# Block kernel with experts: order of the last blocks, reads of the y rows, and whole weight loads

## The chip, the core and the metric

The kernel runs on one core of a Trainium2 chip. The metric is the time of one execution on the device in microseconds (us), the median of three runs. A profiled execution is taken by itself; its instructions are placed in microseconds from the start of its span.

## What is computed

One layer of a hybrid block on x of 512 tokens x 1024: a mixing half (a spatial gate beside stick-breaking attention), then a mixture of experts. All of what is changed lies in the second half:

```python
gates = route(h, w_router, router_bias)          # 64 experts, 8 of them per token, others 0
g = jnp.einsum('sd,edf->sef', hs, w_gate)        # 1024 -> 256 per expert
u = jnp.einsum('sd,edf->sef', hs, w_up)
act = jax.nn.silu(g) * u * gs[:, :, None]
routed = jnp.einsum('sef,efd->sd', act, w_down)  # 256 -> 1024
y = routed + (jax.nn.silu(h @ ws_gate) * (h @ ws_up)) @ ws_down
x = x + ga2 * rmsnorm(y, g_post_ffn)
```

All inputs are float32. The kernel splits an operand into a rounded high part and the rest ("low") and multiplies high x high, high x low and low x high.

## The kernel before, in words

**Blocks.** The experts are done sparsely. A block is one expert with up to 128 of its tokens. Blocks 0 to 63 are the experts in order. Where an expert has more than 128 tokens, further blocks follow at the end; `nover` of them were counted on the chip, and `npair` = m pairs are run. Here m = 2, 68 blocks. Blocks alternate between two sets of tiles (slots s = 0, 1).

**Tables.** `posb` and `vtab` hold a column per block: each token's place in the block and the values that give its row and gate. A fill loop on GpSimd (`fill_step`, L657 and L660) copies the columns of an over-full expert for its further blocks. `eid` names the expert of a block behind the 64th.

**One block.** SyncE loads gate and up weights (1 MB each) into `raw`, in two halves of the inner range: half 0 of gate and up, then half 1 (`load_half`, L472; 4 KB per partition and piece). `refill` issues a half when VectorE has subtracted the same half of the block two before. ScalarE rounds a half to `whi` (`high`, L858), VectorE computes `wlo` = raw - whi (`low`, L1791, semaphore `lo_dve`, two counts per block). GpSimd gathers the token rows (L622); TensorE transposes them (L1001), computes the place tables (L1297) and multiplies gate and up over k = 0 to 7 (`gate_up`, L1317 to L1319), waiting for `lo_dve` before k = 0 and again before k = 4. VectorE forms silu(g) x u x gate (L1798), TensorE transposes it (L1001) and multiplies with the down weights (`down`, L1335 and L1341); these are loaded by ScalarE's queue (L905) and split at L910 and L1815. ScalarE takes the result out (`ysb`, L901) and GpSimd scatters its rows (L630).

**The y rows.** `y_rows` in DRAM has 4096 rows of 1024: row 8 x token + rank, where the rank counts the token's selected experts in the order of their numbers. After the last block SyncE waits for all scatters and reads everything back into `yall` (16 MB, laid over the tiles of the blocks), in 8 transfers: for each row group t of 128 tokens ranks 0 to 3, then ranks 4 to 7 (L526). Then per row group: TensorE sums the shared expert's rows `ysh` and ranks 0, 1, 2, 4 with an identity matrix (`part_sum`, L1421); VectorE adds ranks 5, 6, 7 to rank 3 (L1887), then TensorE's sum (L1889); ScalarE squares the result (L992); VectorE multiplies it by ga2 (L1891), works out the norm's factor (`factor`, L1448 to L1456, with ScalarE's root, L708) and adds to x (L1898). SyncE writes the output (L531).

**Order.** Each engine's order is written out by hand: `step_dve`, `step_act`, `step_pool` and `block_pe` do a part of several neighbouring blocks each. `step_dve` of block b: row table of b-3, place table of b+2, low part of b's token rows, of the down weights of b-2, one-hot of b+3, the low part of the activations of b-2, `low` of b, and `times_up` of b-1. `block_pe` of b: transposes of b+1, tables of b+3, gate/up products of b, down products of b-1. SyncE's queue holds the refills, and after the last one the reads of y.

Of the kernel before, what the change touches and what calls it, by code (L numbers as in the profile page):

```python
# [24 lines left out]
I32 = mybir.dt.int32  # L25
# [29 lines left out]
COLS = E + OVER + 6  # L55
# [3 lines left out]
HC = 1024  # L59
# [3 lines left out]
def block_kernel(nc, x, c, w_ada, b_ada, g_pre_mix, w_in, ln_sgu_g, ln_sgu_b, w_spatial, b_spatial,  # L63
                 g_branch, w_out, g_post_mix, g_pre_ffn, w_router, router_bias, w_gate, w_up,
                 w_down, ws_gate, ws_up, ws_down, g_post_ffn, out):
    with ExitStack() as ctx:
# [19 lines left out]
        yall = at("yall", [P, TT, TOPK, D], F32, 0)  # L86
# [123 lines left out]
        eid = small("eid", [1, E + OVER], I32)  # L210
        offs = small("offs", [P, OVER], F32)
# [114 lines left out]
        scatter_go = sem("scatter_go")  # L326
        gathered = [sem(f"gathered{s}") for s in range(SLOTS)]
# [18 lines left out]
        y_in = [sem(f"y_in{t}_{g}") for t in range(TT) for g in range(2)]  # L346
        ypart_mm = sem("ypart_mm")
        root_set = sem("root_set")
        ysum_ok = sem("ysum_ok")
# [10 lines left out]
        y_v = y_rows.rearrange("(t p r) n -> t p r n", r=TOPK, p=P)  # L360
# [31 lines left out]
        Y_BANK = [0, 2, 6, 0]  # L392
        Y_PE, Y_DVE = (0, 1, 2, 4), (5, 6, 7)
# [38 lines left out]
        def _(sp):  # L432
# [36 lines left out]
            def load_half(e, s, half):  # L469
                cols = slice(half * HC, (half + 1) * HC)  # L470
                for m_, w in enumerate((wg_v, wu_v)):
                    sp.dma_start(raw[:, s, m_, cols], w[bass.ds(e, 1)].rearrange("e p f -> p (e f)")[:, cols])\  # L472
                      .then_inc(gu_in[s][half], 16)

            def load_gate_up(e, s):
                for half in range(2):
                    load_half(e, s, half)
# [26 lines left out]
            def refill(i, s, e):  # L504

                b = num(*after(i, s, -2))
                for half in range(2):
                    sp.wait_ge(lo_dve, b * 2 + (1 + half))
                    load_half(e, s, half)

            with sp.Fori(2, E // 2) as i:
                for s in range(SLOTS):
                    refill(i, s, num(i, s))
            sp.wait_ge(over_ok, 1)
            m = sp.value_load(npair[0:1, 0:1], min_val=0, max_val=OVER // 2)
            with sp.If(m > 0):
                with sp.Fori(E // 2, m + E // 2) as i:
                    for s in range(SLOTS):
                        e = sp.value_load(eid[0:1, bass.ds(num(i, s), 1)], min_val=0, max_val=E - 1)
                        refill(i, s, e)  # L520

            for s in range(SLOTS):
                sp.wait_ge(scattered[s], m * 16 + 16 * (E // 2))
            for t in range(TT):
                for g in range(2):
                    sp.dma_start(yall[:, t, 4 * g:4 * g + 4], y_v[t][:, 4 * g:4 * g + 4]).then_inc(y_in[2 * t + g], 16)  # L526
# [9 lines left out]
        def _(gp):  # L536
# [21 lines left out]
            gp.iota(eid[:, 0:E], [[1, E]], base=0, channel_multiplier=0)  # L558
            then(gp.iota(iote[:, :], [[0, 1]], base=0, channel_multiplier=1, allow_small_or_imprecise_dtypes=True))
# [94 lines left out]
            with gp.If(n > 0):  # L654
                with gp.Fori(0, n) as j:
                    e = gp.value_load(eid[0:1, bass.ds(j + E, 1)], min_val=0, max_val=E - 1)
# [5 lines left out]
            gp.sem_inc(fill_step, 1)  # L662
            gp.wait_ge(fill_step, n * 2 + 1)
            gp.sem_inc(fill_ok, 1)
            step_pool(1, 1)
            m = gp.value_load(npair[0:1, 0:1], min_val=0, max_val=OVER // 2)
# [13 lines left out]
        def _(ac):  # L680
# [171 lines left out]
            def high(i, s, half):  # L852
                ac.wait_ge(gu_in[s][half], i * 32 + 32)
                if half == 0:
                    if not (isinstance(i, int) and i == 0):
                        ac.wait_ge(gu_mm, num(i, s) - 1)
                cols = slice(half * HC, (half + 1) * HC)
                A(whi[:, s, :, cols], raw[:, s, :, cols], ACT.Copy).then_inc(hi_ok, 1)  # L858
# [107 lines left out]
            with ac.Fori(3, E // 2) as i:  # L966
                for s in range(SLOTS):
                    step_act(i, s, 3)
            ac.wait_ge(over_ok, 1)
            m = ac.value_load(npair[0:1, 0:1], min_val=0, max_val=OVER // 2)  # L970
            with ac.If(m > 0):
# [958 lines left out]
```

## Time and profile before

| | us |
|---|---|
| median of 3 runs | 1081.46 (1081.21 to 1082.55) |
| profiled execution, its own time | 1087.6 |
| its span | 1085.9 |
| TensorE busy | 1027.3 |
| VectorE busy | 858.2 |
| ScalarE busy | 648.0 |
| GpSimd busy | 287.3 |

In the profile PE is TensorE's products, PEld its weight loads, DVE VectorE, ACT ScalarE, POOL GpSimd, SP SyncE; L12 is line 12 of the kernel. A float32 product of 128x512 stands as two passes (records). The share of busy time is an average over stages: the mixing half and the routing take the first 350 us, the blocks run to about 1028 us, the sum of the y rows is the rest. PEclk is the clock granted to TensorE as a share of 2.4 GHz. "Idle before" is how long the engine idled before an instruction, and what ended that.

### The profile page before, as it was taken

The page shows a single profiled execution, that of the slowest core. Times are in us where ns is not written, and L with a number is a line of the kernel's source. Part 1 is how long each engine was busy: PE and PEld are TensorE (multiplying, and loading weights), DVE is VectorE, ACT ScalarE, POOL GpSimd, SP SyncE. Part 2 cuts the span into 40 slices and gives each one's busy share as a digit, 9 for nine tenths or more (in the row PEclk, how much of TensorE's full clock was granted, in tenths as well). Part 3 has the DMA queues.
Part 4 walks back from the last instruction along what each step waited for, and adds up shares of the span by engine and source line. Part 5 has one row for each costly group of instructions (what it writes and reads, how often), then busy time and mean ns, then how long its engine had stood idle before and what let it go on. Part 6 is the DMA issues. An engine that isn't in the chain of part 4 may idle for free.

```text
span 1085.9 us, 15632 instructions
## 1 busy us (share of the span) xinstructions
PE 1027.3 (95%) x4668; PEld 744.5 (69%) x4668; DVE 858.2 (79%) x1412; ACT 648.0 (60%) x743; POOL 287.3 (26%) x220
## 2 busy tenths in 40 slices
PE   4998999899998999999999999999999999999866
PEld 0786776568755777777777777777777777777632
DVE  1669766644778898888898899989899999999447
ACT  5334135742443777677677677777677777777501
POOL 1232221540303432222221232233123223322200
PEclk9899998999999999999999999999999999999989
DMA  9666752112344899999999999999999999999297
GB/s 338 253 244 260 262 169 93 61 37 107 103 189 163 311 374 370 364 365 367 384 364 384 356 366 364 380 371 368 365 363 352 350 357 357 354 360 334 84 394 301
DMA packets 87495, 318.67 MB, mean 293 GB/s; under 512 B 19312, under 2 KB 19824, under 8 KB 77360
## 3 DMA queue, kind: packets, MB, share of 16 engines
q1 hardware_dynamic: 53232, 200.30, 50.6%
q10 hardware_dynamic: 11616, 72.66, 17.4%
q0 software_dynamic: 22624, 45.40, 11.3%
q8 instruction: 13, 0.21, 0.1%
q14 instruction: 10, 0.08, 0.0%
HBM read 317.25 MB, written 39.85 MB: 329 GB/s over the span
## 4 chain that ended last, share of the span: by engine, by line
PE 56%; DMA 24%; DVE 11%; ACT 4%; issue 3%; SPq 1%; ACTq 1%; DVEq 0%; POOL 0%; POOLq 0%
DMA raw<-in_w_up_dram 18%; PE ps L1317 7%; PE ps L1319 7%; PE ps L1318 7%; PE ps L1335 6%; PE ps L1091 6%; PE ps L1341 5%; PE ps L1001 5%; DMA yall<-y_rows 4%; DVE wlo L1791 3%; PE ps L1193 2%; ACT whi L858 2%; PE ps L1175 2%; PE ps L1017 2%; PE ps L1142 1%
## 5 line engine op out<-in xcount | busy, mean ns | idle before, releaser
L1791 DVE TENSOR_TENSOR wlo<-raw,whi 128x2048 fp32r<-128x2048 f32 x136 | 307.8, 2287 | 34.0 <-ACT whi L858 34.0
L858 ACT ACTIVATE whi<-raw 128x2048 fp32r<-128x2048 f32 x136 | 261.0, 1920 | 73.2 <-DMA raw<-in_w_up_dram 72.8
L1317 PE MATMUL ps<-whi,hthi 128*128 128x512 f32 x544 | 224.6, 413 | 0.0
L1319 PE MATMUL ps<-whi,htlo 128*128 128x512 f32 x544 | 212.8, 391 | 0.0
L1318 PE MATMUL ps<-wlo,hthi 128*128 128x512 f32 x544 | 212.6, 391 | 0.0
L630 POOL DMA_INDIRECT y_rows<-ysb,idxs x68 | 69.1, 1016 | 461.1 <-DVE idxg L1785 432.4
L622 POOL DMA_INDIRECT hg<-h_rows,idxg x70 | 129.5, 1850 | 70.4 <-DVE idxg L1785 50.2
L901 ACT ACTIVATE ysb<-ps 128x1024 f32<-128x1024 f32 x68 | 69.7, 1025 | 107.2 <-PE ps L1341 107.1
L1335 PE MATMUL ps<-rawd,actt 128*128 128x512 f32 x272 | 127.7, 592 | 1.5 <-ACT actt L894 1.5
L1319 PEld LDWEIGHTS ps<-whi,htlo 128*128 128x128 f32 x544 | 102.1, 188 | 22.8
L1318 PEld LDWEIGHTS ps<-wlo,hthi 128*128 128x128 f32 x544 | 102.6, 189 | 17.0
L1317 PEld LDWEIGHTS ps<-whi,hthi 128*128 128x128 f32 x544 | 102.2, 188 | 17.1
L1805 DVE TENSOR_TENSOR htlo<-ps,hthi 128x1024 fp32r<-128x1024 f32 x68 | 83.3, 1225 | 10.7 <-ACT hthi L890 10.7
L1815 DVE TENSOR_TENSOR wdlo<-rawd,wdhi 128x1024 fp32r<-128x1024 f32 x68 | 82.7, 1216 | 1.5 <-ACT wdhi L910 1.5
L1341 PE MATMUL ps<-wdhi,acth 128*128 128x512 f32 x136 | 80.9, 595 | 0.0
L1335 PEld LDWEIGHTS ps<-rawd,actt 128*128 128x128 f32 x272 | 51.1, 188 | 39.7 <-issue 32.7
L1001 PE MATMUL ps<-ident,hg 128*128 128x128 f32 x552 | 71.7, 273 | 0.5 <-DVE eid L1754 0.4
L910 ACT ACTIVATE wdhi<-rawd 128x1024 fp32r<-128x1024 f32 x68 | 72.1, 1061 | 0.0
L890 ACT ACTIVATE hthi<-ps 128x1024 fp32r<-128x1024 f32 x68 | 69.4, 1021 | 2.8 <-PE ps L1001 2.8
L1001 PEld LDWEIGHTS ps<-ident,hg 128*128 128x128 f32 x552 | 64.3, 140 | 9.4 <-DVE eid L1754 0.5
L1770 DVE TENSOR_SCALAR s_onehot<-iotab,posb 128x128 bf16<-128x128 bf16 x284 | 62.1, 284 | 0.0
L1473 DVE SCALAR_TENSOR_TENSOR acc<-ada,sc_col,acc 128x1024 f32<-128x1024 f32 x35 | 53.0, 1515 | 3.8 <-DMA ada<-in_w_ada_dram 2.7
(270 smaller groups left out, 1614.7 us busy)
## 6 DMA issues: line engine op xcount, KB each, us to landing
raw<-in_w_gate_dram SPq DMA_DIRECT2D x136, 512.0 KB
raw<-in_w_up_dram SPq DMA_DIRECT2D x136, 512.0 KB
rawd<-in_w_down_dram ACTq DMA_DIRECT2D x66, 1024.0 KB
ada<-in_w_ada_dram SPq DMA_DIRECT2D x24, 1024.0 KB, 8.6
yall<-y_rows SPq DMA_DIRECT2D x8, 2048.0 KB, 22.9
wraw<-in_w_in_dram POOLq DMA_DIRECT2D x8, 1024.0 KB, 5.7
woraw<-in_w_out_dram SPq DMA_DIRECT2D x16, 256.0 KB, 2.8
xs<-in_x_dram SPq DMA_DIRECT2D x4, 512.0 KB, 6.0
```

Of the source, the lines that this page charges most:

```text
L622: gp.indirect_dma_start(out=hg[s][:, :, :].rearrange("p k q -> p (k q)"), out_offset=None, in_=h_rows, in_offset=bass.IndirectOffsetOnAxis ...
L858: A(whi[:, s, :, cols], raw[:, s, :, cols], ACT.Copy).then_inc(hi_ok, 1)
L910: A(wdhi[s][:, :, :], rawd[:, s, :, 0:DC], ACT.Copy).then_inc(wdhi_ok, 1)
L1001: return pe.transpose(o, i, ident[:, :])
L1317: mm(out_, hthi[s][:, k, :], hi, start=(k == 0), stop=False)
L1318: mm(out_, hthi[s][:, k, :], lo, start=False, stop=False)
L1319: ins = mm(out_, htlo[s][:, k, :], hi, start=False, stop=(k == KD - 1))
L1335: mm(bank(5), actt[:, k, :], rawd[:, s, k, DC:D], start=(k == 0), stop=(k == KF - 1))
L1341: ins = mm(bank(4), a_[:, k, :], w, start=(k == 0 and j == 0), stop=(k == KF - 1 and j == 2))
L1791: V.tensor_tensor(wlo[s][:, :, c0:c1], raw[:, s, :, c0:c1], whi[:, s, :, c0:c1].bitcast(F32), ALU.subtract).then_inc(lo_dve, 1)
L1805: V.tensor_tensor(htlo[s][:, :, :], bank(0, 2).rearrange("p (k q) -> p k q", k=KD), hthi[s][:, :, :].bitcast(F32), ALU.subtract).then_inc( ...
L1815: V.tensor_tensor(wdlo[:, s, :, 0:DC], rawd[:, s, :, 0:DC], wdhi[s][:, :, :].bitcast(F32), ALU.subtract)\
```

## The change

- The further blocks of over-full experts come after block 55, before the last eight experts (`MID` = 56, `LASTE` = 8). To this end GpSimd copies the table columns of experts 56 to 63 behind those of the further blocks, and their numbers into `eid`; from block 56 on SyncE and ScalarE read the expert from `eid`, and VectorE's `onehot` takes columns shifted by 8.
- Gate and up are loaded, rounded and subtracted whole, one after the other, instead of in two halves of both. TensorE waits for both subtractions before k = 0.
- The y rows are read rank by rank into tiles `yr0` to `yr7` that lie over tiles of the last blocks: rank 0 after block 66's subtractions (numbers as with 68 blocks), ranks 1 and 2 after its gate/up products, rank 3 after block 67's subtractions, ranks 4 and 5 after its gate/up products, ranks 6 and 7 after the last down products, by row group. Before the read of rank r SyncE also waits until the block of expert 56 + r is scattered.
- VectorE adds the shared rows to rank 0, then ranks 1, 2, 3, 5. TensorE sums rank 4, VectorE's sum, ranks 6 and 7. ScalarE squares TensorE's sum out of PSUM. The product with ga2 reads PSUM too and stands behind the variance.

```diff
@@ names and tiles
+LASTE = 8
+MID = E - LASTE
+COLS = E + OVER + LASTE + 6
-        yall = at("yall", [P, TT, TOPK, D], F32, 0)
+        yr = [at(f"yr{r}", [P, TT, D], F32, (0, 48, 96, 16, 64, 80, 32, 112)[r] * KB) for r in range(TOPK)]
-        y_v = y_rows.rearrange("(t p r) n -> t p r n", r=TOPK, p=P)
+        y_v = y_rows.rearrange("(t p r) n -> p t r n", r=TOPK, p=P)
-        Y_BANK = [0, 2, 6, 0]
-        Y_PE, Y_DVE = (0, 1, 2, 4), (5, 6, 7)
+        Y_BANK = [0, 2, 4, 6]
+        Y_DVE = (1, 2, 3, 5)
@@ SyncE
+            def load_one(e, s, m_):
+                sp.dma_start(raw[:, s, m_, :], (wg_v, wu_v)[m_][bass.ds(e, 1)].rearrange("e p f -> p (e f)"))\
+                  .then_inc(gu_in[s][m_], 16)
...
+            def rank_done(r):
+
+                pairs = (MID + r) // 2
+                sp.wait_ge(scattered[r % 2], m * 16 + 16 * (pairs + 1))
+                sp.sem_inc(read_go, 1)
+
+            def read_rank(r):
+                sp.dma_start(yr[r][:, :, :], y_v[:, :, r]).then_inc(y_in[r], 16)
+
+            for r in range(4):
+                rank_done(r)
+            sp.wait_ge(lo_dve, m * 4 + 2 * (E - 2) + 2)
+            sp.sem_inc(read_go, 1)
+            read_rank(0)
+            sp.wait_ge(gu_mm, m * 2 + (E - 1))
+            sp.sem_inc(read_go, 1)
+            read_rank(1)
+            read_rank(2)
+            sp.wait_ge(lo_dve, m * 4 + 2 * (E - 1) + 2)
+            sp.sem_inc(read_go, 1)
+            read_rank(3)
+            sp.wait_ge(gu_mm, m * 2 + E)
+            sp.sem_inc(read_go, 1)
+            rank_done(4)
+            read_rank(4)
+            rank_done(5)
+            read_rank(5)
+            sp.wait_ge(dn_mm, m * 2 + E)
+            sp.sem_inc(read_go, 1)
+            rank_done(6)
+            rank_done(7)
+            for t in range(TT):
+                for r in (6, 7):
+                    sp.dma_start(yr[r][:, t, :], y_v[:, t, r]).then_inc(y_last[t], 16)
@@ GpSimd, behind the fill loop
+            gp.tensor_copy(posb[:, :, bass.ds(m * 2 + E, LASTE)], posb[:, :, MID:E]).then_inc(fill_step, 1)
+            gp.tensor_copy(vtab[:, :, bass.ds(m * 2 + E, LASTE), :].rearrange("p t b v -> p t (b v)"),
+                           vtab[:, :, MID:E, :].rearrange("p t b v -> p t (b v)")).then_inc(fill_step, 1)
+            gp.tensor_copy(eid[:, bass.ds(m * 2 + MID, LASTE)], elast[:, :]).then_inc(fill_step, 1)
@@ ScalarE
+                A(whi[:, s, m_, :], raw[:, s, m_, :], ACT.Copy).then_inc(hi_ok, 1)
...
-                ac.wait_ge(ysum_ok, t + 1)
-                A(junk[:, :], yall[:, t, 3, :], ACT.Square, accum_out=stat[:, ST_S, t:t + 1]).then_inc(sumsq, 1)
+                ac.wait_ge(ypart_mm, t + 1)
+                A(junk[:, :], bank(Y_BANK[t], 2), ACT.Square, accum_out=stat[:, ST_S, t:t + 1]).then_inc(sumsq, 1)
@@ TensorE
                 if k0 == 0:
                     pe.wait_ge(htlo_ok, num(i, s) + 1)
+                    pe.wait_ge(lo_dve, num(i, s) * 2 + 2)
                 for k in range(k0, k1):
-                    if k == 0 or k == KH:
-                        pe.wait_ge(lo_dve, num(i, s) * 2 + 1 + k // KH)
...
+            def add_rows(t, rows, first=False, last=False):
+                for hf in range(2):
+                    ins = mm(bank(Y_BANK[t] + hf), ident[:, :], rows[:, hf * 512:(hf + 1) * 512], start=first, stop=last)
+                return ins
+
+            pe.wait_ge(y_in[4], 16)
+            for t in (0, 1, 3, 2):
+                if t == 2:
+                    pe.wait_ge(y_ok, m * 2 + E)
+                add_rows(t, yr[4][:, t, :], first=True)
+            for t in range(TT):
+                pe.wait_ge(dsum_ok, t + 1)
+                add_rows(t, yr[0][:, t, :])
+                pe.wait_ge(y_last[t], 32)
+                add_rows(t, yr[6][:, t, :])
+                add_rows(t, yr[7][:, t, :], last=True).then_inc(ypart_mm, 1)
@@ VectorE
+            def shared_rank0(t):
+                y = yr[0][:, t, :]
+                then(V.tensor_tensor(y, y, ysh[t][:, :], ALU.add))
+
+            v.wait_ge(y_in[0], 16)
+            shared_rank0(0)
+            shared_rank0(1)
             times_up(last, 1)
             down_low(last, 1)
             rows_of(last, 0)
+            shared_rank0(2)
             act_low(last, 1)
             rows_of(last, 1)
+            shared_rank0(3)
+            for r in Y_DVE:
+                v.wait_ge(y_in[r], 16)
+                for t in range(TT):
+                    y = yr[0][:, t, :]
+                    ins = V.tensor_tensor(y, y, yr[r][:, t, :], ALU.add)
+                    if r == Y_DVE[-1]:
+                        ins.then_inc(dsum_ok, 1)
+                    else:
+                        then(ins)
+            def weighted(t):
+
+                v.wait_ge(ypart_mm, t + 1)
+                return V.tensor_tensor(yr[0][:, t, :], bank(Y_BANK[t], 2), ga2[:, :], ALU.mult)
```

## Rows read from the trace of the kernel before

**Rows 1.** Chain that ended last, from 900 us on: start us, us, what.
```profile
1030.29 2.06 DMA y_rows<-ysb,idxs
...
1035.76 38.50 DMA yall<-y_rows
```

**Rows 2.** Busy us of each engine by stretch, then PEclk, DMA share, GB/s.
```profile
403.00:626.00 223.00, 218.79 (x1060) 165.63 (x1058) 193.62 (x330) 162.37 (x177) 58.18 (x44) 1.00 0.98 368
...
715.00:796.00 81.00, 79.58 (x387) 60.46 (x386) 70.37 (x121) 59.48 (x65) 21.07 (x16) 1.00 0.98 367
...
796.00:1014.00 218.00, 218.00 (x1058) 166.28 (x1057) 202.01 (x332) 161.03 (x177) 66.16 (x44) 1.00 0.94 343
```

**Rows 3.** Timeline of PE and DVE: start us, us, engine line op, idle before.
```profile
614.51 0.48 PE L1317 MATMUL ps<-whi,hthi 128*128 128x512 f32 x1
...
615.31 2.29 DVE L1791 TENSOR_TENSOR wlo<-raw,whi 128x2048 fp32r<-128x2048 f32 x1 [3.50 <-ACT whi L858]
...
626.02 0.48 PE L1317 MATMUL ps<-whi,hthi 128*128 128x512 f32 x1
...
989.30 4.49 DVE L1791 TENSOR_TENSOR wlo<-raw,whi 128x2048 fp32r<-128x2048 f32 x2
...
994.38 0.48 PE L1317 MATMUL ps<-whi,hthi 128*128 128x512 f32 x1
```

**Rows 4.** Waits of the whole run: us in total, times, longest us.
```profile
DVE wlo L1791 <- ACT whi L858: 34.0, 27, 3.5
```

**Rows 5.** DMA by queue, 403 to 615 us: packets, MB, share.
```profile
q1 hardware_dynamic: 12079, 43.99, 56.7%
...
q10 hardware_dynamic: 3024, 22.02, 26.8%
```

**Rows 6.** DMA by queue, 1034 to 1074 us.
```profile
q1 hardware_dynamic: 1224, 16.71, 98.9%
```

**Rows 7.** Timeline of the last blocks, POOL, DVE, PE and ACT.
```profile
995.56 1.02 POOL L630 DMA_INDIRECT y_rows<-ysb,idxs  x1 [6.65 <-DVE idxg L1785]
...
1001.50 2.28 DVE L1791 TENSOR_TENSOR wlo<-raw,whi 128x2048 fp32r<-128x2048 f32 x1
...
1020.03 1.88 PE L1335 MATMUL ps<-rawd,actt 128*128 128x512 f32 x4
...
1020.51 1.05 ACT L910 ACTIVATE wdhi<-rawd 128x1024 fp32r<-128x1024 f32 x1
...
1030.29 0.96 POOL L630 DMA_INDIRECT y_rows<-ysb,idxs  x1 [4.07 <-ACT ysb L901]
```

**Rows 8.** DMA issues of the whole run: KB each, us to landing.
```profile
rawd<-in_w_down_dram ACTq DMA_DIRECT2D x66, 1024.0 KB
...
y_rows<-ysb,idxs POOLq DMA_INDIRECT x68, 8.1
```

**Rows 9.** Timeline of DVE after the last block.
```profile
1024.94 0.43 DVE L1820 TENSOR_TENSOR actl<-actt,acth 128x256 fp32r<-128x256 f32 x1 [2.06 <-ACT acth L895]
...
1044.71 3.74 DVE L1887 TENSOR_TENSOR yall<-yall 128x1024 f32<-128x1024 f32 x3 [19.28 <-DMA yall<-y_rows]
```

**Rows 10.** Timeline of PE after the last block.
```profile
1039.78 9.26 PE L1421 MATMUL ps<-yall,ident 128*128 128x512 f32 x16 [9.65 <-DMA yall<-y_rows]
...
1050.59 7.03 PE L1421 MATMUL ps<-yall,ident 128*128 128x512 f32 x16
```

**Rows 11.** Busy us by stretch after the last block; the clock as PEclk.
```profile
1036.00:1040.00 4.00, 0.22 (x1) 0.23 (x2) 0.00 (x0) 0.00 (x0) 0.00 (x0) 0.50 1.05 446
```

**Rows 12.** Timeline of the last row group's end, ACT and DVE.
```profile
1079.38 1.06 ACT L992 ACTIVATE junk<-yall 128x1024 f32<-128x1024 f32 x1 [8.40 <-DVE yall L1889]
...
1082.04 1.41 DVE L1898 SCALAR_TENSOR_TENSOR xs<-yall,rs,xs 128x512 f32<-128x512 f32 x2
```

**Rows 13.** Timeline of POOL around the fill of the over-full blocks.
```profile
360.73 2.27 POOL L660 COPY vtab<-vtab  x1
...
374.50 1.02 POOL L630 DMA_INDIRECT y_rows<-ysb,idxs  x1 [6.49 <-DVE idxg L1785]
```

## What is predicted

> **What bounds the kernel now.** I read the chain that ended last first, then the busy time by stretch, then the timelines of the last blocks. The chain's end [rows 1] shows a tail that starts when the last block's scatter is done: 1030.29 + 2.06 = 1032.35 us. Only then does SyncE read the 16.8 MB of y rows back, 38.50 us of pure transfer in the chain, and the span ends 53.5 us after the scatter landed. In that time TensorE and VectorE mostly wait or add rows. Before it, over 68 blocks, TensorE is full: from 796 to 1014 us it is busy for 218.00 of 218.00 us at a period of 9.91 us, while from 403 to 626 and from 715 to 796 us it loses 4.2 and 1.4 us with the DMA engines at 0.98 [rows 2]. So in the middle TensorE bounds and the weight loads come close to it; there is at most 5.6 us to win there. What the tail holds is much more.
>
> **Tail, part by part.** The change reads rank r of all 512 tokens (2.10 MB) as soon as the tile under it is used up. That is allowed since rank r of a token can't lie in a later expert than 56 + r, and the last eight blocks are now experts 56 to 63.
>
> 1. First issue. Rank 0 waits for block 66's second weight subtraction, which ends at 1001.50 + 2.28 = 1003.8 us [rows 7]; the scatter of block 63, the last of the four that SyncE waits for, is issued at 995.56 [rows 7] and lands some 8.1 us later [rows 8], at the same time. SyncE's refills are all issued 10 us before, so nothing of them stands behind the new waits. So 28.5 us of the 53.5 us head start are won in principle.
>
> 2. What has to flow before rank 4 is in. TensorE begins with rank 4, and SyncE's queue runs in order, so ranks 0 to 4 come first: 5 x 2.10 = 10.5 MB. Beside them go two down loads of 1.05 MB [rows 8] and three scatters of blocks 64 to 66, 64 rows x 4 KB = 0.26 MB each: 13.4 MB in all. The latency from issue to use: the first VectorE add began at 1044.71 [rows 9], 12.4 us after 1032.35, for 4.19 MB, which at the rate of [rows 6] are 9.9 us; 2.4 us remain.
>
> 3. The rate. Reads of y rows before had runs of 16 KB and made 16.71 MB / (0.989 x 40 us) = 422 GB/s [rows 6]. The new ones have runs of 4 KB, as the halves of the gate and up loads do: 43.99 / (0.567 x 212) = 366 GB/s while they mix with scatters and gathers [rows 5]. These two are the bounds. I take 395, the middle: 4 KB runs, but little beside them. Rank 4 is in at 1003.8 + 2.4 + 33.9 = 1040.1 us (1037.9 by the fast bound, 1042.8 by the slow one). The Trainium skill (DMA: Bandwidth & Descriptors, Specifications) gives about 358 GB/s as the HBM limit of a core; by it rank 4 would be in at 1043.6 us and the end 3.5 us later than in my sum. Behind that rule: the trace does not agree, the tail's row shows 422 GB/s.
>
> 4. TensorE then adds rank 4 for four row groups, 16 passes. It will have idled some 11 us after the last down product. Before, after a similar wait the granted clock was 0.50, the 1.2 GHz level, when the adds began [rows 11], and the first 16 passes took 9.26 us where a later 16 took 7.03 us [rows 10]. So rank 4 ends at 1049.3 us.
>
> 5. Next, per row group: VectorE's sum, rank 6, rank 7, 12 passes, 48 in all: 3 x 7.03 = 21.1 us, to 1070.5 us. Are their inputs there? VectorE adds the shared rows in the gaps of the last block, then 16 adds (ranks 1, 2, 3, 5) of 3.74 / 3 = 1.25 us [rows 9] from about 1026.6 us, after the last act_low and one more shared add. The adds of ranks 1 to 3 run to 1041.6 us. Rank 5 lands at 1003.8 + 2.4 + 15.7 MB / 0.395 = 1046.0 us and the first sum is ready at 1047.3, 2 us before TensorE asks. Ranks 6 and 7 of group 0 land near 1049 us, of group 3 near 1057 us, where TensorE asks at 1067. The last scatter is issued at 1030.29 [rows 7]; amid the reads it may land several us later than before, but SyncE's own queue is full until 1046. So **TensorE is late next**: its adds come one behind the other from 1040 us.
>
> 6. After TensorE: before, from the start of the last Square (1079.38) to the span's end took 6.5 us [rows 12]. Square now reads PSUM instead of the sum. VectorE's add from PSUM (1.2 us) goes away. The product with ga2, which ran beside Square, now comes after it, inside the wait for the root: +1.0 us. So 7.5 us: the end is 1070.5 + 7.5 = 1078.0 us against 1085.9: **7.9 us less** (bounds of the rate: 10.0 and 5.2; a clock that stays up adds 2.2).
>
> The down load of block 67, issued after the down products of block 65, now shares the engines with ranks 1 to 3. Its first use was at 1020.51 us [rows 7]. If it is 5 us late, the last down product moves from 1028 to 1033, and TensorE waits for rank 4 until 1040 anyway: nothing.
>
> **Middle.** (a) Gate and up are loaded whole, 8 KB runs instead of 4 KB. The down loads have had 8 KB runs all along: 22.02 / (0.268 x 212) = 388 GB/s against 366 for the gate and up halves in the same stretch [rows 5]. That is 5.4 us instead of 5.7 us of DMA time per block, 0.3 of about 10. In the two late stretches blocks take 10.1 us instead of 9.87, so this gain alone is about what is lacking; bounds zero and the full 5.6 us. (b) TensorE now waits for both subtractions before its first gate/up product. In an undisturbed block the second ends at 989.30 + 4.49 = 993.79, 0.6 us before the products start at 994.38 [rows 3]: hidden, and this slack is all the cover there is. In a late block it isn't: at 615.31 + 2.29 = 617.6 the second one ends 3.1 us after the start at 614.51 [rows 3]. Before, only the products from k = 4 waited (the next block's began 11.5 us on, at 626.02, 1.6 us late); now all of the 3.1 us stand. All waits of this kind sum to 34.0 us in 27 places [rows 4]. I don't expect this sum: while the loads set the pace, the blocks' ends are given by the DMA rate, and starting later costs the lost cover (2.5 to 3 us) once per stretch, two stretches, 5 us. With (a) taking most of the lateness away, I put (a) and (b) together at **3 us less**, between 5.6 less and 5 more.
>
> **Costs at nothing.** Over-full blocks ahead of the last eight: the same 68 blocks, the same loads. The experts read from a table in 12 blocks instead of 4: SyncE and ScalarE did it in the four last ones before, in the stretch without a stall [rows 2]. Three more copies and an iota on GpSimd: the copies there took up to 2.27 us [rows 13], it idles 6.5 us before its scatter one block on, and the gather behind them is needed a block later still.
>
> **Sum.** 7.9 + 3 = 10.9 us. The profiled execution has 1087.6 us around a span of 1085.9; the median of the runs is 1081.46, 6 us less. The tail's part should carry over; of the stalls in the middle fewer may exist there, which I leave within the range. 1081.46 - 10.9 = **1070.6 us**.
>
> **Rivals.**
> - R1, the lost cover outweighs the wide loads: middle 2 to 5 us more, tail as above: 1075.5 to 1079. For it: the slack of 0.6 us [rows 3]. Against: the 388 against 366 GB/s. Chance 0.14.
> - R2, TensorE pays every late subtraction, since its delay moves the next block's subtractions and loads too: 34.0 us less the 5.6 already lost, +28: about 1102. It decides once the middle loses over 8 us. Against: the last third has no late block. Chance 0.05.
> - R3, the strided rank reads are slow, **ending slower than before**: rows of 4 KB at 32 KB from token to token and 4 MB from row group to row group. At half my rate (0.198 MB/us) the 16.8 MB take 85 us, with 8 us for the rest; ranks 6 and 7 would land at 1099, and 3.5 + 7.5 us of adds and end give 1110 in the span: about 1106. It decides below 277 GB/s. Against: the before reads step by 32 KB between tokens too. The Trainium skill (DMA: Bandwidth & Descriptors, Latency and other measured facts) reports copies falling to about half at a row pitch of 4 MiB per partition; no run here shows that, and the 4 MB step here lies between row groups of one partition. Chance 0.05.
> - R4, better than the sum: fast bound of the rate, clock kept up, stalls all gone and a little more: 18 to 22 us less, 1060 to 1063.5. Chance 0.07.
> - R5, the early reads don't start early, since a scatter's landing holds SyncE behind the whole chain of waits: each wait is in order, so one late scatter delays all ranks behind it. 5 to 8 us of the tail's gain lost: 1076 to 1080. Chance 0.04.
> - Forecast: tail 5 to 12 less, middle 0 to 5.6 less. Chance 0.65.
>
> About 0.2% (2.2 us) is what a measurement of this kernel can tell from no change. Faster: 0.65 + 0.07 + most of R1 and R5 = 0.86; same 0.04; slower 0.10. The range, 1063 to 1078, holds the forecast and most of R1, and leaves out R2, R3, nearly all of R4.
>
> **What would show it.** Step 1: first y read issued near 1004 us, before the last block's products. Steps 2 and 3: y reads landing in order at 395 GB/s. Step 4: TensorE's rank 4 adds begin near 1040 us at a low clock. Step 5: from 1049 us TensorE without a gap for 21 us, VectorE's waits for DMA before it. Middle: second weight subtractions ending before the products in most blocks, TensorE idle under 3 us between 403 and 1014. I am wrong if TensorE waits for VectorE or the DMA after 1050 us, or if its idle time in the middle grows.

## The result, and the profile after

| | before | after |
|---|---|---|
| median, runs on the same chip | 1082.01 (1081.21 to 1083.09, 4 runs) | 1071.05 (1069.88 to 1075.07, 4 runs) |
| ratio | | 0.9905, 95% interval 0.9877 to 0.9932 |
| profiled execution, its own time | 1087.6 | 1075.07 |
| its span | 1085.9 | 1073.0 |

The kernel is faster by 11.0 us at the medians; forecast were 10.9 us and 1070.6. To see where they came from I cut each span at two marks that every kernel here has: the start of the gate/up products of block 2 and of the last block. What lies between them, 66 blocks, I call the middle, what follows the tail.

Timeline of TensorE after, the two marks and the adds of the y rows (start us, us, engine line operation, idle before):

```profile
363.59 0.47 PE L1348 MATMUL ps<-whi,hthi 128*128 128x512 f32 x1
...
1009.30 0.47 PE L1348 MATMUL ps<-whi,hthi 128*128 128x512 f32 x1
...
1035.94 29.68 PE L1442 MATMUL ps<-yr,ident 128*128 128x512 f32 x64 [11.80 <-DMA yr<-y_rows]
```

Before, the same marks stand at 363.54 and 1014.21 us, with the span's end at 1085.9. So the middle went from 650.7 to 645.7 us, **5.0 less**, and the tail from 71.7 to 63.7 us, **8.0 less**. The forecast was 3 and 7.9. Together that is 13.0 us in one pair of profiles (the spans differ by 12.9); the medians show 11.0, with an interval of 7 to 13.

One profile is one execution. In the six kernels that are the same up to the last block (this one and e5 to e9 below) the middle took 642.9 to 645.8 us. With e1 that makes seven kernels with whole loads, at 642.9 to 647.1; the two with the loads and waits of before took 650.7 and 651.2 (e4). So a gain in the middle is clear, its size only to some 2 us. The tail repeats better: 71.3 to 71.7 us in the four kernels that have the tail of before, 63.1 (e6) and 64.2 (e8) in two that have the changed one but for one detail.

**The middle after.** Busy us by stretch (PE, PEld, DVE, ACT, POOL, each with its instructions, then PEclk, DMA share, GB/s), to be laid beside [rows 2]:

```profile
403.00:626.00 223.00, 221.99 (x1079) 169.35 (x1078) 203.96 (x339) 164.75 (x180) 67.89 (x46) 1.00 0.97 376
...
715.00:796.00 81.00, 80.89 (x392) 61.58 (x391) 74.34 (x128) 60.06 (x68) 24.39 (x17) 1.00 0.98 377
796.00:1014.00 218.00, 218.00 (x1058) 166.47 (x1057) 199.39 (x323) 157.72 (x174) 65.43 (x43) 1.00 0.93 349
```

TensorE's idle time in the two late stretches fell from 4.2 to 1.0 and from 1.4 to 0.1 us. The costliest groups of instructions on the page (busy us, mean ns of one, idle before) no longer show a wait at the subtractions, where [rows 4] had 34.0 us, nor at the roundings:

```profile
L1821 DVE TENSOR_TENSOR wlo<-raw,whi 128x2048 fp32r<-128x2048 f32 x136 | 305.2, 2285 | 0.0
L891 ACT ACTIVATE whi<-raw 128x2048 fp32r<-128x2048 f32 x136 | 261.4, 1923 | 0.0
```

DMA by queue, 403 to 615 us (packets, MB, share of 16 engines), beside [rows 5]: gate and up on q1 now move at 45.07 / (0.547 x 212) = 389 GB/s, where the 4 KB halves made 366, and close to the 388 of the down loads on q10 before.

```profile
q1 hardware_dynamic: 6189, 45.07, 54.7%
```

**The tail after.** Chain that ended last, from 1000 us on (start us, us, what), beside [rows 1]. Where 38.50 us of transfer stood in front of everything, 20.38 us stand now, and then TensorE works:

```profile
1015.52 20.38 DMA yr<-y_rows
1035.94 29.70 PE ps L1442 x64
1065.67 1.12 ACT junk L1024 x2
...
1066.97 1.14 DVE yr L1935
...
1069.10 0.75 DVE xs L1942
```

SyncE, its waits from 988 to 1001.2 us (us in total, times, longest), then its timeline:

```profile
SPq L527 <- DMA y_rows<-ysb,idxs: 10.5, 2, 9.6
```

```profile
1000.60 0.38 SPq L530 DMA_DIRECT2D yr<-y_rows  x1
...
1005.47 3.69 SPq L530 DMA_DIRECT2D yr<-y_rows  x3
```

The first read is issued at 1000.60 us, the next three from 1005.47 on. VectorE's timeline shows what the first one waited for besides the scatters, and the adds that follow:

```profile
994.38 4.49 DVE L1821 TENSOR_TENSOR wlo<-raw,whi 128x2048 fp32r<-128x2048 f32 x2
...
1023.50 15.12 DVE L1926 TENSOR_TENSOR yr<-yr,yr 128x1024 f32<-128x1024 f32 x12
1041.80 4.63 DVE L1926 TENSOR_TENSOR yr<-yr,yr 128x1024 f32<-128x1024 f32 x4 [3.18 <-DMA yr<-y_rows]
```

Block 66's second subtraction ends at 994.38 + 4.49 = 998.87 us, 1.7 us before the read is issued: in between, SyncE was still held by the scatter of block 63.

DMA by queue, 1004 to 1040 us: the reads on q1 made 12.76 / (0.888 x 36) = 399 GB/s.

```profile
q1 hardware_dynamic: 3218, 12.76, 88.8%
q10 hardware_dynamic: 144, 1.05, 7.5%
```

Stretches around the start of TensorE's adds; the third figure from the right is the granted clock:

```profile
1030.00:1035.00 5.00, 0.00 (x0) 0.00 (x0) 4.86 (x5) 0.00 (x0) 0.00 (x0) 0.50 1.03 413
1035.00:1040.00 5.00, 4.06 (x5) 1.85 (x6) 3.55 (x3) 0.00 (x0) 0.00 (x0) 0.51 1.02 407
1040.00:1045.00 5.00, 5.00 (x13) 2.23 (x12) 3.20 (x3) 0.00 (x0) 0.00 (x0) 1.00 1.03 411
```

The clock is at 0.50, the 1.2 GHz level, after 11.80 us of idling and while the first adds run: 5 passes in 4.06 us. From 1040 us on it is at 2.4 GHz: 13 passes in 5 us.

### The profile page after: what moved, and what is told of

Read it like the earlier page. It is cut to its first block, busy times and chain, and to the rows that moved or that the text cites. A ratio compares the mean times of both kernels' runs of the same rounds, so it can differ in the third digit from the quotient of the medians.

```text
span 1073.0 us, 15239 instructions
## 1 busy us (share of the span) xinstructions
PE 1019.2 (95%) x4652; PEld 743.2 (69%) x4652; DVE 870.5 (81%) x1416; ACT 644.7 (60%) x743; POOL 299.5 (28%) x224
## 4 chain that ended last, share of the span: by engine, by line
PE 80%; DMA 9%; DVE 7%; ACT 2%; issue 1%; ACTq 0%; SPq 0%; POOL 0%; DVEq 0%; POOLq 0%
PE ps L1348 11%; PE ps L1350 11%; PE ps L1349 11%; PE ps L1366 10%; PE ps L1033 8%; PE ps L1372 8%; PE ps L1123 6%; DMA hg<-h_rows,idxg 6%; PE ps L1442 3%; PE ps L1225 2%; DMA yr<-y_rows 2%; PE ps L1207 2%; PE ps L1049 2%; PE ps L1174 1%; PE ps L1285 1%
## 5 line engine op out<-in xcount | busy, mean ns | idle before, releaser
L661 POOL DMA_INDIRECT y_rows<-ysb,idxs x68 | 69.0, 1015 | 444.9 <-DVE idxg L1816 389.6
L653 POOL DMA_INDIRECT hg<-h_rows,idxg x70 | 140.3, 2005 | 71.0 <-DVE idxg L1816 50.5
## 6 DMA issues: line engine op xcount, KB each, us to landing
raw<-in_w_gate_dram SPq DMA_DIRECT2D x68, 1024.0 KB, 10.9
raw<-in_w_up_dram SPq DMA_DIRECT2D x68, 1024.0 KB, 12.9
rawd<-in_w_down_dram ACTq DMA_DIRECT2D x66, 1024.0 KB, 10.1
```

Of the source, the lines that this page charges most:

```text
L653: gp.indirect_dma_start(out=hg[s][:, :, :].rearrange("p k q -> p (k q)"), out_offset=None, in_=h_rows, in_offset=bass.IndirectOffsetOnAxis ...
```

## Experiments

Two questions: do the middle and the tail gain what the spans say, each by its own part of the change, and which resource sets the tail? Nine kernels were run. All do the whole computation; e6 adds products that are not needed. The runs of before beside them had medians of 1082.19 us (e1 to e4), 1082.40 (e5 to e8) and 1082.75 (e9).

**e1, the wide loads alone.** The kernel before, with whole loads of gate, then up, their roundings and subtractions whole, and TensorE waiting for both subtractions.

```diff
-            def load_half(e, s, half):
-                cols = slice(half * HC, (half + 1) * HC)
-                for m_, w in enumerate((wg_v, wu_v)):
-                    sp.dma_start(raw[:, s, m_, cols], w[bass.ds(e, 1)].rearrange("e p f -> p (e f)")[:, cols])\
-                      .then_inc(gu_in[s][half], 16)
+            def load_half(e, s, m_):
+                sp.dma_start(raw[:, s, m_, :], (wg_v, wu_v)[m_][bass.ds(e, 1)].rearrange("e p f -> p (e f)"))\
+                  .then_inc(gu_in[s][m_], 16)
...
+                    pe.wait_ge(lo_dve, num(i, s) * 2 + 2)
                 for k in range(k0, k1):
-                    if k == 0 or k == KH:
-                        pe.wait_ge(lo_dve, num(i, s) * 2 + 1 + k // KH)
```

> The kernel before with the whole gate and up loads and the one wait for both subtractions; order of blocks, y reads and sums as before. Theory (8 KB runs make the loads fast enough, nothing is lost by the wait): VectorE never waits for a rounded half (0 instead of 34.0 us), TensorE idles under 2 us between 403 and 1014 us, span 1080 to 1082, 3 to 5 us less than before. Rival (the middle's gain in the changed kernel came from the new order of the blocks): waits of 30 us or more remain and the time is that of before or 2 to 5 us more.

Measured: 1078.17 us, ratio 0.9958 (0.9941 to 0.9975), 4.0 us less at the medians. The page's group of the subtractions, and the stretch 403 to 626 us:

```profile
L1786 DVE TENSOR_TENSOR wlo<-raw,whi 128x2048 fp32r<-128x2048 f32 x136 | 305.2, 2284 | 0.0
```

```profile
403.00:626.00 223.00, 221.57 (x1067) 167.44 (x1066) 202.56 (x333) 163.85 (x179) 59.95 (x45) 1.00 0.97 373
```

The waits are gone and TensorE idles 1.4 instead of 4.2 us. The middle took 647.1 us (before 650.7), the tail 71.4 (before 71.7). So this part by itself makes most of the middle's gain and next to nothing in the tail.

**e2, the lost cover alone.** The kernel before, halves as they were, only TensorE's wait changed:

```diff
+                    pe.wait_ge(lo_dve, num(i, s) * 2 + 2)
                 for k in range(k0, k1):
-                    if k == 0 or k == KH:
-                        pe.wait_ge(lo_dve, num(i, s) * 2 + 1 + k // KH)
```

> The kernel before, only that TensorE waits for both weight subtractions before its first gate/up product; loads in 4 KB halves as before. Theory (the DMA engines set the pace in the late stretches, the lost cover is paid once per stretch): 2 to 6 us more than before. Rival (R2 of the prediction: each late subtraction is paid for): 20 to 28 us more. Second rival (a late TensorE leaves the DMA engines time to catch up, nothing is paid): within 1 us of before.

Measured: 1089.07 us, ratio 1.0061 (1.0038 to 1.0084), 6.9 us more than the median of before; the middle grew by 4.3 us to 655.0. Waits of its whole run:

```profile
PE ps L1316 <- DVE wlo L1790: 10.0, 8, 1.9
...
DVE wlo L1790 <- ACT whi L858: 16.2, 10, 2.9
```

TensorE waits in 8 places, 10.0 us in total. The 34.0 us of late subtractions do not turn into 34 us of waits of TensorE, and VectorE's own are down to 10 places and 16.2 us. This refutes R2's price (28 us) and bears out that of step (b) of the middle, about 5 us.

**e3, the width of the runs.** As e1, but each matrix comes in two transfers with 4 KB per partition: gate, gate, up, up.

```diff
-                sp.dma_start(raw[:, s, m_, :], (wg_v, wu_v)[m_][bass.ds(e, 1)].rearrange("e p f -> p (e f)"))\
-                  .then_inc(gu_in[s][m_], 16)
+                for half in range(2):
+                    cols = slice(half * HC, (half + 1) * HC)
+                    sp.dma_start(raw[:, s, m_, cols],
+                                 (wg_v, wu_v)[m_][bass.ds(e, 1)].rearrange("e p f -> p (e f)")[:, cols])\
+                      .then_inc(gu_in[s][m_], 16)
```

> As the kernel with whole loads only, but each matrix in two transfers with runs of 4 KB: gate first, then up, one wait, narrow runs. If the width of the runs makes the gain: VectorE's waits for ScalarE come back (over 20 us) and the time is as with both waits alone. If it is that gate is loaded whole before up (or fewer waits at SyncE): 3 to 5 us less than before, as with the whole loads.

Measured: 1082.69 us, ratio 0.9997 (0.9979 to 1.0016), the same as before. Waits of its whole run:

```profile
DVE wlo L1789 <- ACT whi L858: 17.7, 15, 2.6
...
PE ps L1316 <- DVE wlo L1789: 8.6, 10, 1.9
```

Against e1 the pieces are half as wide, and there are four transfers of 512 KB per block instead of two of 1 MB: 1082.69 - 1078.17 = 4.5 us. So the wide loads pay; whether by their 8 KB runs or by their fewer and larger transfers no run here tells apart. Against e2 the width, the transfers and the wait for both subtractions are the same. Only the order differs (gate whole before up, and so too the roundings and subtractions), and e3 is 6.4 us faster by time (2.9 us in the middles, 652.1 and 655.0). So the order counts too: it takes back what the merged wait cost. How it does so stays open, since the waits of the two are nearly alike (17.7 and 16.2, 8.6 and 10.0 us). e1's 4.0 us are then the sum of three steps: + 6.9 for the merged wait (e2), - 6.4 for the order, - 4.5 for the wide loads.

**e4, the tail alone.** The changed kernel with halves, two roundings over both and the two waits of before.

```diff
-                sp.dma_start(raw[:, s, m_, :], (wg_v, wu_v)[m_][bass.ds(e, 1)].rearrange("e p f -> p (e f)"))\
-                  .then_inc(gu_in[s][m_], 16)
+                cols = slice(half * 1024, (half + 1) * 1024)
+                for m_, w in enumerate((wg_v, wu_v)):
+                    sp.dma_start(raw[:, s, m_, cols], w[bass.ds(e, 1)].rearrange("e p f -> p (e f)")[:, cols])\
+                      .then_inc(gu_in[s][half], 16)
...
-                    pe.wait_ge(lo_dve, num(i, s) * 2 + 2)
                 for k in range(k0, k1):
+                    if k == 0 or k == KH:
+                        pe.wait_ge(lo_dve, num(i, s) * 2 + 1 + k // KH)
```

> The changed kernel with the loads, the subtractions and TensorE's two waits in halves again, as before. Theory (tail and middle add up): 8 us less than before, about 1074, 3 us more than the changed kernel; the last gate/up product ends near 1020 us and from there to the end it takes 58 us. Rival (the new order of blocks alone changed the middle): within 1 us of the changed kernel.

Measured: 1076.06 us, ratio 0.9929 (0.9903 to 0.9955). The subtractions' group on its page has the waits of before again:

```profile
L1826 DVE TENSOR_TENSOR wlo<-raw,whi 128x2048 fp32r<-128x2048 f32 x136 | 307.9, 2286 | 37.6 <-ACT whi L894 37.6
```

The forecast was 8 us less than before. Its middle took 651.2 us, as before (650.7), its tail 65.8, 2.1 more than the changed kernel's. Most of that lies in the reads: the one of rank 0 took 11.9 us from issue to landing instead of 9.1, and rank 4's adds begin 28.4 us after the last block's products instead of 26.6. Why the reads are slower behind the halves wasn't tested. At the medians e4 saves 6.1 and e1 4.0 us, 10.1 together, by the ratios 7.7 and 4.5, 12.2 together; the whole change saves 11.0 by the one and 10.3 by the other. Within the intervals the two parts add up.

**e5, no early start.** The changed kernel, with all reads behind the last scatter; VectorE's adds of the shared rows go behind its work on the last block, as they would lock up otherwise.

```diff
             sp.sem_inc(read_go, 1)
-            read_rank(0)
...
             rank_done(6)
             rank_done(7)
+            read_rank(0)
+            read_rank(1)
+            read_rank(2)
+            read_rank(3)
+            read_rank(4)
+            read_rank(5)
```

> The changed kernel, but all reads of the y rows are issued after the last scatter; ranks, tiles, sums and loads as changed. Theory (the tail's gain is the early start, and TensorE's adds come one behind the other after rank 4): rank 4 is in at about 1057 us, then 9.3 + 21.1 + 7.5 us: a span of about 1095, 20 to 23 us more than the changed kernel and so about 9 more than before. Rival (the gain is the new sharing of the sums, the early start is hidden): within 5 us of the changed kernel.

Measured: 1090.74 us, ratio 1.0078 (1.0057 to 1.0098). TensorE's timeline, and DMA by queue from 1030 to 1050 us, where nothing but these reads runs:

```profile
1051.58 29.45 PE L1442 MATMUL ps<-yr,ident 128*128 128x512 f32 x64 [33.12 <-DMA yr<-y_rows]
```

```profile
q1 hardware_dynamic: 2051, 8.19, 102.4%
```

The early start is worth 1090.74 - 1071.05 = 19.7 us (18.7 by the ratios, as the two were not measured side by side), and the rest of the tail's change without it loses more than it brings: the kernel is slower than before although it keeps the wide loads. TensorE starts 47.1 us after the last block's products began, instead of 26.6. And the reads alone, 4 KB at a time with 32 KB from token to token and 4 MB from row group to row group, run at 8.19 / 20 = 409 GB/s. R3 is refuted: counted the same way, without the share, the 16 KB reads of [rows 6] made 16.71 / 40 = 418 GB/s.

**e6, the clock kept up.** The changed kernel, with 10 needless products (20 passes) between the last down product and the wait for rank 4; their result is overwritten.

```diff
+            for n in range(10):
+                mm(bank(0), ident[:, :], ga2[:, 0:512], start=True, stop=True)
             pe.wait_ge(y_in[4], 16)
```

> The changed kernel with ten needless products (20 passes) between the last down products and the wait for rank 4, into a bank that is overwritten. Theory (the clock's fall costs 2.2 us in the rank 4 adds, and the rest of the tail follows TensorE): 16 passes take 7.1 us instead of 9.2, the span is 2 us less. Rival (VectorE's sums or the last reads hold the start of the row groups): 0 to 0.5 us less, TensorE then waits for VectorE at 1043 us.

Measured: 1071.12 us, ratio 0.9892 (0.9871 to 0.9913), no gain over the changed kernel. TensorE's timeline, VectorE's, and the stretches around the start of the adds:

```profile
1021.03 8.74 PE L1446 MATMUL ps<-ga,ident 128*128 128x512 f32 x20
1032.34 29.43 PE L1442 MATMUL ps<-yr,ident 128*128 128x512 f32 x64 [2.56 <-DMA yr<-y_rows]
```

```profile
1038.45 4.63 DVE L1928 TENSOR_TENSOR yr<-yr,yr 128x1024 f32<-128x1024 f32 x4 [2.79 <-DMA yr<-y_rows]
```

```profile
1032.00:1034.00 2.00, 1.66 (x4) 0.95 (x5) 1.97 (x2) 0.00 (x0) 0.00 (x0) 0.93 1.02 406
1034.00:1036.00 2.00, 2.00 (x3) 0.73 (x3) 1.63 (x2) 0.00 (x0) 0.00 (x0) 0.50 1.02 408
1036.00:1038.00 2.00, 2.00 (x4) 0.73 (x3) 0.00 (x0) 0.00 (x0) 0.00 (x0) 0.71 1.03 412
```

The idle time before the adds fell from 11.80 to 2.56 us, but the clock was not kept up: it is at 2.4 GHz when the adds begin, falls to 1.2 GHz within 2 us although TensorE works, and is back between 1036 and 1038 us. So the 64 passes take 29.43 instead of 29.68 us, and the experiment does not do what it was made for. What a steady clock would give I can only work out: the 80 passes of e7 below take 34.49 us, 0.431 each, so 64 would take 27.6, 2.1 us less. VectorE's first sum would be in time for that: here it is ready at 1038.45 + 4.63 / 4 = 1039.6 us, 7.3 us after the adds began, as the first 16 passes would end (7.03 us in [rows 10]).

**e7, another sharing.** If TensorE's 64 passes behind rank 4 set the end, it should begin with rank 1, which lands earlier. TensorE adds ranks 1, 3, 4, then 7 and VectorE's sum (80 passes); VectorE adds ranks 2, 5, 6.

```diff
-        Y_DVE = (1, 2, 3, 5)
+        Y_DVE, Y_PE = (2,), (1, 3, 4)
...
-            pe.wait_ge(y_in[4], 16)
-            for t in (0, 1, 3, 2):
-                if t == 2:
-                    pe.wait_ge(y_ok, m * 2 + E)
-                add_rows(t, yr[4][:, t, :], first=True)
+            for r in Y_PE:
+                pe.wait_ge(y_in[r], 16)
+                for t in (0, 1, 3, 2):
+                    if r == Y_PE[0] and t == 2:
+                        pe.wait_ge(y_ok, m * 2 + E)
+                    add_rows(t, yr[r][:, t, :], first=(r == Y_PE[0]))
```

> The changed kernel with the adds shared differently: TensorE takes ranks 1, 3 and 4 as they come from 1024 us on, then only rank 7 and VectorE's sum per row group; VectorE takes ranks 2, 5 and 6. Theory (TensorE's 21 us of adds behind rank 4 set the end): rank 4 done at 1045 us, four groups of 3.5 us to 1059, end at 1067 us, 6 us less than the changed kernel. Rival (the DMA engines or VectorE set the end): 0 to 2 us less, TensorE waits for VectorE's sums after 1045 us.

Measured: 1066.72 us, ratio 0.9857 (0.9841 to 0.9874), 4.3 us below the changed kernel: it is faster than both kernels. The forecast was 6 us. TensorE's timeline, then VectorE's from its last add of rank 6 on:

```profile
1021.72 34.49 PE L1442 MATMUL ps<-yr,ident 128*128 128x512 f32 x80
```

```profile
1047.74 1.23 DVE L1932 TENSOR_TENSOR yr<-yr,yr 128x1024 f32<-128x1024 f32 x1 [0.94 <-DMA yr<-y_rows]
...
1048.95 1.21 DVE L1937 TENSOR_TENSOR yr<-ps,ga 128x1024 f32<-128x1024 f32 x1
...
1052.56 1.22 DVE L1937 TENSOR_TENSOR yr<-ps,ga 128x1024 f32<-128x1024 f32 x1
...
1056.17 1.22 DVE L1937 TENSOR_TENSOR yr<-ps,ga 128x1024 f32<-128x1024 f32 x1
...
1059.79 1.22 DVE L1937 TENSOR_TENSOR yr<-ps,ga 128x1024 f32<-128x1024 f32 x1
```

TensorE has 80 passes instead of 64 and is done at 1056.2 us, 51.1 us after the last block's products began, instead of 56.3. The bound is now VectorE: its last adds wait for the DMA and it then needs 3.6 us per row group, one behind the other. The tail took 60.8 us. Part of the gain may be the clock: TensorE's adds start at 2.4 GHz here, without a wait in front of them.

**e8, rank 0 earlier.** The changed kernel, where the read of rank 0 waits for the scatter of block 60 only (experts 56 to 59 are blocks 60 to 63).

```diff
-            for r in range(4):
-                rank_done(r)
+            rank_done(0)
...
             read_rank(0)
+            for r in range(1, 4):
+                rank_done(r)
```

> The changed kernel, but the read of rank 0 waits for the scatter of block 60 alone; the waits for blocks 61 to 63 stand behind it. Theory (the first read was held 1.6 us by the scatter of block 63, and all reads follow in order): the first read is issued at 999 us, rank 4 is in 1.6 us earlier, the span is 1 to 1.6 us less. Rival (ranks 1 to 5 are held by their own waits): rank 4 is in at the same time, no change.

Measured: 1069.98 us, ratio 0.9879 (0.9857 to 0.9902), the same as the changed kernel. SyncE's timeline and TensorE's:

```profile
993.73 10.16 SPq L530 DMA_DIRECT2D yr<-y_rows  x4
```

```profile
1004.00 0.47 PE L1349 MATMUL ps<-whi,hthi 128*128 128x512 f32 x1
...
1030.67 30.14 PE L1443 MATMUL ps<-yr,ident 128*128 128x512 f32 x64 [11.65 <-DMA yr<-y_rows]
```

The read starts 10.3 us before the last block's products instead of 8.7, as the forecast had it for the change. But the adds of rank 4 begin 26.7 us after them, as in the changed kernel (26.6). The earlier read moved hardly anything ahead. Counted from 12 us before the last block's products, all queues had moved 3.54 MB by 1 us before them (changed kernel: 3.47 MB), and 6.94 MB by 8 us after them (6.96 MB). Ranks 1 and 2 can't be issued before TensorE has left their tiles: rank 1 goes out 3.8 us before the last products in both kernels, and in the changed one the DMA share dips between that and the last products:

```profile
1008.30:1009.30 1.00, 1.00 (x13) 0.97 (x12) 0.99 (x3) 0.69 (x1) 0.00 (x0) 1.00 0.72 258
```

That the issue of rank 1 sets when rank 4 is in fits both kernels, but no run moved it by itself.

**e9, VectorE relieved.** As e7, with rank 3 back on VectorE and rank 6 of the last two row groups on TensorE. The edit is shown against the changed kernel.

```diff
-        Y_DVE, Y_PE = (2,), (1, 3, 4)
+        Y_DVE, Y_PE = (2, 3), (1, 4)
...
+                if t >= 2:
+                    add_rows(t, yr[6][:, t, :])
                 add_rows(t, yr[7][:, t, :])
```

> The kernel with the adds shared differently, one step further: VectorE, which idled 11.8 us before rank 5, also takes rank 3, and TensorE takes rank 6 of the last two row groups. Theory (in the first balance VectorE's chain of sums and norms, 3.6 us per row group behind 1049 us, set the end): 2 to 3 us less than the first balance, 1064 us, the end 7.5 us after TensorE's last pass. Rival (the work is balanced already, the last reads set the end): within 0.5 us of the first balance, 1066.7 us.

Measured: 1066.57 us (1063.36 to 1069.49), ratio 0.9858 (0.9834 to 0.9882). TensorE's timeline:

```profile
1019.22 7.03 PE L1442 MATMUL ps<-yr,ident 128*128 128x512 f32 x16
...
1029.03 7.13 PE L1442 MATMUL ps<-yr,ident 128*128 128x512 f32 x16 [2.77 <-DMA yr<-y_rows]
1036.49 17.48 PE L1442 MATMUL ps<-yr,ident 128*128 128x512 f32 x40 [0.33 <-DMA yr<-y_rows]
```

In its profile the tail is 58.5 us, 2.3 less than in e7. TensorE's last pass ends at 1053.97 us, 51.1 us after the last block's products began as in e7, but the span now ends 7.4 us behind it instead of 9.7: VectorE's chain of sums no longer sets the end. By time it is no faster than e7, in runs 6 us apart, and 1064 was forecast. Whether the 2.3 us are real is not decided.

## Why the prediction was right

The sum held: 10.9 us forecast, 11.0 measured, and both parts were found by themselves (e1 and e4). That it held to 0.1 us is luck: the interval is 7 to 13 us, the one pair of profiles shows 13.0, and in the middle the sum has no term for the order of the loads (6.4 us), which took back a cost of the merged wait that was larger than forecast. The mechanism of the tail, an early start of the reads and then TensorE's adds one behind the other, is shown by e5 and e7. Step by step:

- **Tail, step 1, first issue.** Forecast: at the subtractions of block 66, 10.4 us before the last block's products. Measured: 8.7 us before, held 1.7 us by the scatter of block 63. I had both ending at the same time; the scatter took longer to land. e8 takes 1.6 of the 1.7 us back and shows that they were worth nothing.
- **Steps 2 and 3, data and rate.** Forecast 395 GB/s with rank 4 in 25.9 us after the products' start (1040.1 - 1014.21). Measured 399 GB/s and 26.6 us. From the first issue to the adds of rank 4 I had 2.4 + 33.9 = 36.3 us, and it took 1035.94 - 1000.60 = 35.3. So a start 1.7 us late and a flow 1.0 us shorter leave 0.7 us; the rate makes 0.3 of that 1.0, the rest I can't assign. What the sum lacked is that the reads do not flow freely from rank 0 on, since ranks 1 and 2 wait for their tiles (e8). The Trainium skill (HBM Reference, Specifications (TRN2)) adds to the 358 GB/s that I weighed that a core which streams alone goes well above it; the 399 to 422 GB/s of this case's tails agree with that.
- **Step 4, rank 4 at a low clock.** Forecast a granted clock of 0.50 and 9.3 us for 16 passes. Measured 0.50 until 1040 us, and 9.1 us for them. That a clock kept up adds 2.2 us (R4) was not shown: e6 didn't keep it up. From e7's passes it would be 2.1.
- **Step 5, TensorE is late next.** Forecast 9.3 + 21.1 = 30.4 us for 64 passes without a gap; measured 29.68 us. VectorE's wait for rank 5 was forecast and was 3.18 us. e7 confirms the reading: fewer passes behind rank 4 end the kernel earlier, until VectorE sets the end.
- **Step 6, the end.** Forecast 7.5 us from TensorE's last pass to the span's end; measured 1073.0 - 1065.6 = 7.4.
- **The down load of block 67.** ScalarE waited 2.60 us for it at 1018.30, and TensorE 2.17 us for the transposed activations at 1020.78. It cost nothing, as forecast, since TensorE waits for rank 4 afterwards.
- **Middle.** Forecast 3 us less, between 5.6 less and 5 more; measured 5.0 less in the spans. The mis-sized step is (a) and (b) together, for which I had put 3 us instead of 5.6 less. TensorE's idle time fell by 4.5 us, the loads made 389 against 366 GB/s, as (a) had it, and no subtraction waits any more, so the lost cover of (b) had nothing left to cost. But the experiments divide the gain otherwise than I did. By medians the merged wait costs 6.9 us (e2), where I had 5; the wide loads bring 4.5 (e1 against e3), which I put down to the 8 KB runs alone though the transfers are larger too; and the order of the loads, for which I had no term at all, brings 6.4 (e3 against e2).
- **From the profile to the median.** I took the profiled execution of before as 6 us over the median and left open that some stalls of the middle are its own. Most of the difference probably lies ahead of the blocks instead: block 2 began at 363.54 us, where seven of the eleven profiles have 358 to 360.
- **Rivals.** R1 and R2 fall with e1 and the middle after, R3 with e5, R5 with step 1: its mechanism is there, 1.7 us of it, at no cost. R4's fast bounds weren't reached: 422 GB/s was not, and the clock fell. That the parts at no cost (order of the blocks, copies on GpSimd) are free is borne out only in sum: e4's middle is within 0.5 us of before.

## What to carry to other kernels

A read-back at the end of a kernel can be cut by the time at which its data are final, if the work is ordered so that late data are few and each piece has a tile that is free by then; here the early start was worth 20 us, and the new adds without it would have lost. After that, order each engine's adds by arrival and give the engine that waits for the late piece the least work behind it. Where an engine's wait for two halves is merged into one, see to the loads as well: the same merge cost 7 us with the halves in the old order, nothing with pieces as narrow that bring one matrix after the other, and came with a gain of 4 us with whole loads.

## What the runs showed of the hardware

- The first 360 us differ between executions of kernels that are all but the same there. Block 2's products start at 363.54 in the profile of before, 363.59 after, 363.11 in e6, but between 358.17 and 361.36 in the other eight. Here is the first mark of e1:

```profile
359.27 0.48 PE L1313 MATMUL ps<-whi,hthi 128*128 128x512 f32 x1
```

  That is up to 5 us without a change, more than some of the effects looked for; e6 and e8, with the same code up to there and run on the same chip, differ by 4.9. Marks inside the span were needed to see the effects in one profile. Most of it arises near 107 us, at a product of the mixing half that waits for weights. Here after and e8, then TensorE's stretch from 105 to 115 us in each:

```profile
106.66 0.50 PE L1123 MATMUL ps<-h1hi,wphi 128*128 128x512 f32 x1 [3.31 <-DVE wplo L1529]
...
103.97 0.50 PE L1124 MATMUL ps<-h1hi,wphi 128*128 128x512 f32 x1 [1.23 <-DVE wplo L1530]
```

```profile
105.00:115.00 10.00, 8.34 (x30) 6.75 (x31) 9.73 (x7) 1.55 (x3) 3.14 (x2) 0.83 0.78 253
...
105.00:115.00 10.00, 10.00 (x46) 8.27 (x45) 7.49 (x5) 1.79 (x3) 3.38 (x3) 1.00 0.83 256
```

  The three late profiles (before, after, e6) have a wait of 3.2 to 3.3 us there and a granted clock of 0.83 in the 10 us, e8 has 1.23 us and 1.00; e2 and e7 lie between, with 2.5 us and 1.00. Why the weights come later is not known. This can also be most of why the two profiled executions, before and after, lie some 4 to 6 us above the medians of their runs.
- The granted clock can fall while TensorE works: in e6 it was 0.50 from 1034 to 1036 us, under 4 us into a run of passes, after only 2.56 us without work and 8.74 us of passes before that. In e7, where the adds follow the last down product at once, it was 0.67 from 1015 to 1020 us, with a wait of 2.59 us in it, and 0.99 from 1020 to 1025.
- Reads of 4 KB pieces at 32 KB steps, with 4 MB between row groups, ran at 409 GB/s (e5), beside 418 for the 16 KB pieces of before. The Trainium skill (DMA: Bandwidth & Descriptors, Latency and other measured facts) reports copies at half rate or less when the rows of one transfer lie 4 MiB apart from partition to partition. No run here has that pattern, and a 4 MB step inside a partition did not bring the loss.
- The loads' width and size mattered more among the mixed traffic of the blocks than in a tail where little else runs: 366 and 389 GB/s for halves of 4 KB and whole loads of 8 KB per partition there, 409 and 418 for pieces of 4 and 16 KB here, with transfers of 2 MB in both.
